# Gate tiles of the retention heads as 2x2 blocks with seven products, the retention's units behind them, and the branch sums kept in memory

## What is computed

```python
h = rmsnorm(x, p['norm_pre_mix']) * (1 + sc1) + sh1
q, k, v, g, xr, gr = jnp.split(h @ p['w_in'], SPLITS, axis=-1)
...
o, s_new = retention(q, k, v, s_ret.astype(f32))     # 4 heads, DK 256, DV 512
o = (o - mu) * lax.rsqrt(var + GN_EPS)
ret_y = (o.reshape(B, T, D_RET_V) * p['ret_gn_w'] * jax.nn.silu(g.astype(f32))).astype(dt)
branch_ret = ret_y @ p['w_br_ret']
...
mixed = (ga * branch_ret + gb * branch_rnn) @ p['w_out']
```

## Time and profile before

| | |
|---|---|
| Median of 3 runs | 1374.01 us (1373.72 to 1374.78) |
| The profiled execution | 1375.0 us, span 1373.2 us |
| PE busy | 1336.7 us (97% of the span), granted clock 0.99 |
| PE weight loads busy | 1263.0 us (92%) |
| DVE busy | 815.3 us (59%) |
| ACT busy | 569.0 us (41%) |
| POOL busy | 206.9 us (15%) |
| DMA | mean 138 GB/s; queue of POOL 44.44 MB, queue of SP 141.80 MB |

### The profile page before, as it was taken

One profiled execution on the slowest core, in us unless ns is written; L12 is line 12 of the kernel. 1 busy time (PEld: TensorE's weight loads), 2 busy tenths in 40 slices (PEclk: granted clock), 3 DMA queues, 4 the chain that ended last, 5 costly groups with the idle time before them and its releaser, 6 DMA issues.

```text
span 1373.2 us, 24780 instructions
## 1 busy us (share of the span) xinstructions
PE 1336.7 (97%) x10380; PEld 1263.0 (92%) x10380; DVE 815.3 (59%) x1159; ACT 569.0 (41%) x847; POOL 206.9 (15%) x324
## 2 busy tenths in 40 slices
PE   6999999999999999999999999999899999999997
PEld 3899999988998898899889898999899999999996
DVE  4559888622353594268437734784787888853223
ACT  4667778211222321232224223426555666543221
POOL 1122232000114122301320131000011121100001
PEclk8999999999999999999999999999999999999998
DMA  9412122583424434524442353227054766743323
GB/s 371 172 62 93 63 77 78 207 334 126 178 77 161 154 109 150 178 90 144 148 159 72 137 181 126 78 78 265 2 165 123 183 165 173 181 126 102 95 85 66
DMA packets 61630, 189.91 MB, mean 138 GB/s; under 512 B 6608, under 2 KB 10192, under 8 KB 61136
## 3 DMA queue, kind: packets, MB, share of 16 engines
q1 hardware_dynamic: 44880, 141.80, 29.9%
q0 software_dynamic: 15488, 44.44, 12.5%
q10 hardware_dynamic: 1152, 2.10, 0.4%
HBM read 164.76 MB, written 23.55 MB: 137 GB/s over the span
## 4 chain that ended last, share of the span: by engine, by line
PE 77%; issue 7%; DVE 7%; DMA 4%; ACT 3%; SPq 1%; POOL 1%; DVEq 0%; ACTq 0%; POOLq 0%
PE ps L935 49%; PE ps L1360 14%; PE ps L944 5%; PE ps L1200 2%; DMA out_rs<-state 1%; PE ps L987 1%; PE ps L1183 1%; DMA ada_raw<-in_w_ada 1%; PE ps L1212 1%; PE ps L1244 1%; PE ps L1230 1%; PE ps L1086 1%; DMA raw<-in_w_out 1%; SPq L846 1%; DVE w_lo L1879 1%
## 5 line engine op out<-in xcount | busy, mean ns | idle before, releaser
L935 PE MATMUL ps<-h_hi,w_hi 128*128 128x272 f32 x1520 | 322.1, 293 | 4.5 <-DVE w_lo L1879 3.7
L935 PE MATMUL ps<-h_hi,w_lo 128*128 128x272 f32 x1520 | 315.3, 289 | 0.0
L935 PE MATMUL ps<-h_lo,w_hi 128*128 128x272 f32 x1520 | 314.5, 288 | 0.0
L1879 DVE TENSOR_TENSOR w_lo<-raw,w_hi 128x1024 fp32r<-128x1024 f32 (+2 forms) x154 | 183.9, 1198 | 190.3 <-ACT w_hi L1445 188.6
L935 PEld LDWEIGHTS ps<-h_hi,w_hi 128*128 128x128 f32 x1520 | 241.0, 189 | 16.3 <-issue 9.0
L1445 ACT ACTIVATE w_hi<-raw 128x1024 fp32r<-128x1024 f32 (+2 forms) x154 | 157.6, 1024 | 216.8 <-PE ps L935 116.9
L935 PEld LDWEIGHTS ps<-h_lo,w_hi 128*128 128x128 f32 x1520 | 239.7, 189 | 0.0
L935 PEld LDWEIGHTS ps<-h_hi,w_lo 128*128 128x128 f32 x1520 | 238.4, 190 | 0.0
L2175 DVE SCALAR_TENSOR_TENSOR state<-state,ps 128x512 f32<-128x512 f32 x64 | 41.0, 682 | 97.5 <-PE ps L1244 97.3
L935 PE MATMUL ps<-a_hi,w_hi 128*128 128x272 f32 x308 | 64.0, 289 | 0.2 <-DVE w_lo L1879 0.2
L2592 POOL DMA_DIRECT2D s_raw<-in_w_fin x18 | 15.6, 865 | 321.7 <-DMA s_raw<-in_w_fin 321.7
(11 more groups left out here) (311 smaller groups left out, 2762.3 us busy)
## 6 DMA issues: line engine op xcount, KB each, us to landing
raw<-in_w_head SPq DMA_DIRECT2D x48, 512.0 KB, 3.9
state<-in_state POOLq DMA_DIRECT2D x32, 512.0 KB, 4.6
out_rs<-state POOLq DMA_DIRECT2D x32, 512.0 KB, 4.4
raw<-in_w_rnn SPq DMA_DIRECT2D x24, 512.0 KB, 3.5
ada_more<-in_w_ada SPq DMA_DIRECT2D x23, 512.0 KB, 7.8
raw<-in_w_fin SPq DMA_DIRECT2D x20, 512.0 KB, 5.4
s_raw<-in_w_fin SPq DMA_DIRECT2D x36, 256.0 KB, 5.6
s_raw<-in_w_fin POOLq DMA_DIRECT2D x36, 256.0 KB, 4.9
```

The lines of the kernel that those rows point to most:

```text
L935: mm = nc.tensor.matmul(dst[:, half, :], a, b[:, half * HALF:(half + 1) * HALF], start=first and j == 0, stop=last and j == 2)
L1879: V.tensor_tensor(lo[:, 0:cols], raw_slab(i)[0][:, 0:cols], hi[:, 0:cols].bitcast(F32), ALU.subtract).then_inc(lo_ready, 1)
```

## The change

The four gate tiles of a head become two *pairs*. A pair is written as a 2x2 block product (two weight tiles by two halves of the columns, with the depth halved as well) and computed with seven products of 12 matmuls each. In this text P1 to P7 are the seven products in PE's order, and pair (h, i) is pair i of head h. P1 and P4 use the slab A, P2 and P5 the slab s13, P3 and P6 the slab s24, P7 the half slab a22. P3 adds into P1's bank, P5 and P7 too, P6 into P2's; ACT copies intermediate results out (`copy_head`) first, so P3 waits for copy 1, P5 and P6 for copy 3, P7 for copy 4.

The sums of weight blocks in s13 are made by two SP loads and two accumulating POOL loads into the one buffer `s_head`; those in s24 by two DVE additions in place, after the low part of s13 has been taken. The sums of the input are made once, in head 0, on DVE and ACT; for them the normalised input is written to memory early (`kept_h`) and read back, and the split sums lie where `gbr` and `acc` lay, so `gbr` is written to memory and the branch sums are kept there too: ACT copies each branch tile to one of 4 buffers (`send`), and POOL sends it to memory with an adding DMA (`add_branch`). Two of these buffers lie in `vf`, where the pairs' copies go as well, and two in `cosin`, which is read again in each head. At the end POOL reads `gbr` and `acc` back.

The units that stood behind g0 and g1 now all stand behind P7 of pair 0, those of g2 and g3 behind P7 of pair 1, on all engines. The diff, cut to its core (SP and the plan, PE, ACT, DVE, POOL):

```diff
+HEAD_PRODUCTS = (("q", "A", 0, "B11"), ("t", "s13", 0, "XC"), ("q", "s24", 0, "XA"), ("s", "A", 1, "B21"),
+                 ("q", "s13", 1, "XB"), ("t", "s24", 1, "B22"), ("q", "a22", 0, "XD"))
+SENT = 4
...
-    return tiles + [("g", e) for e in range(ET)]
+    return tiles + [("pair", i) for i in range(ET // 2)]
...
+        for name, key in slabs.items():
+            pl.add_slab(key, BLOCK if name == "a22" else COLS)
+        for side in range(2):
+            pl.add_tile(("pair", h, i, side))
+        for n, (_, name, _, _) in enumerate(HEAD_PRODUCTS):
+            pl.step(slabs[name])
+            pl.product_end[(h, i, n + 1)] = pl.steps
+        for part in range(2):
+            for u in after[("g", 2 * i + part)]:
+                unit(h, u)
...
+            def load_blocks_of_pair(kind, h, i):
+                below = w["w_head"][h, 8 + 2 * i + 1]
+                if kind == "s13":
+                    if (h, i) != (0, 0):
+                        last = pl.kinds["s24"][pair_number(h, i) - 1]
+                        sp.wait_ge(lo_ready, last + 1)
+                    for s in range(2):
+                        sp.dma_start(s_head[:, s, :], below[:, 0:BLOCK]).then_inc(s_head_in, 16)
+                elif kind == "a22":
+                    if i:
+                        sp.wait_ge(lo_ready, pl.slab[("a22", h, i - 1)] + 1)
+                    else:
+                        sp.wait_ge(q_ready, h + 1)
+                    sp.dma_start(head_a22, below[:, BLOCK:2 * BLOCK]).then_inc(a22_in, 16)
...
+            sp.dma_start(kept_h, x_in[:]).then_inc(h_saved, 16)
...
-            sp.dma_start(cosin[:], w["cosin"]).then_inc(cosin_in, 16)
+            sp.wait_ge(h_saved, again(1))
+            for part in range(2):
+                ks = slice(part * KD // 2, (part + 1) * KD // 2)
+                sp.dma_start(h_again[:, ks, :], kept_h[:, ks, :]).then_inc(h_back, 16)
+                load_to(pl.slab[("v", 0, 2 + part, "w", 0)])
             for h in range(H):
+                load_to(pl.slab[("v", h, ET - 1, "w", 0)])
+                if h:
+                    wait_product(sp, h - 1, 1, PRODUCTS)
+                sp.dma_start(cosin[:], w["cosin"]).then_inc(cosin_in, 16)
...
+            def gate_pair_of_head(h, i, after):
+                for side in range(2):
+                    claim(("pair", h, i, side))
+                slabs, number, used = pair_slabs(h, i), pair_number(h, i), set()
+                for n, (bank, name, side, x) in enumerate(HEAD_PRODUCTS):
+                    pe.wait_ge(lo_ready, pl.slab[slabs[name]] + 1)
+                    if x[0] == "X" and number == 0:
+                        pe.wait_ge(x_ready, ("XC", "XB", "XA", "XD").index(x) + 1)
+                    if n in (2, 4, 5, 6):
+                        pe.wait_ge(gate_copied, 4 * number + {2: 1, 4: 3, 5: 3, 6: 4}[n])
+                    hi, lo, _ = parts_of(pl.slab[slabs[name]])
+                    dst = ps[:, pair_bank(h, i, bank), 0:HALF]
+                    x_hi_block, x_lo_block = x_block(h_hi, hx_hi, x), x_block(h_lo, hx_lo, x)
+                    for k in range(KD // 2):
+                        at = side * BLOCK + k * P
+                        whi, wlo, xh, xl = hi[:, at:at + P], lo[:, at:at + P], x_hi_block[:, k, :], x_lo_block[:, k, :]
+                        for j, (a, b) in enumerate(((whi, xh), (whi, xl), (wlo, xh))):
+                            mm = nc.tensor.matmul(dst, a, b, start=bank not in used and k == 0 and j == 0,
+                                                  stop=k == KD // 2 - 1 and j == 2, skip_group_check=True)
+                    mm.then_inc(multiplied, 1)
+                    used.add(bank)
+                for u in after[("g", 2 * i)] + after[("g", 2 * i + 1)]:
+                    unit(h, u)
...
+            def send(h, m):
+                uses = KD // SENT * h + m // SENT
+                if uses:
+                    act.wait_ge(acc_added[m % SENT], 16 * uses)
+                if m == 0:
+                    act.wait_ge(v3_ready, ET * (h + 2))
+                    act.wait_ge(q_ready, h + 2)
+                evacuate(("br", h, m), sent(m))
+            def all_sent(h):
+                for i in range(SENT):
+                    act.wait_ge(acc_added[i], 16 * (KD // SENT) * h)
...
+            def copy_head(h, i, n, product, bank):
+                wait_product(act, h, i, product)
+                do(A(head_copied(n), ps[:, pair_bank(h, i, bank), 0:HALF], ACT.Copy), gate_copied, wait=False)
+            def gate_pair_of_head(h, i, after):
+                first, number = first_of_pair(h, i), pair_number(h, i)
+                split_to(first + 2)
+                if i == 0:
+                    act.wait_ge(q_ready, h + 1)
                     if h:
-                        act.wait_ge(r_ready, ET * h)
-                    evacuate(key, gs[:, i, :], ACT.Silu)
+                        all_sent(h)
+                    else:
+                        act.wait_ge(v3_ready, ET)
+                split_to(first + 3)
+                copy_head(h, i, 0, 1, "q")
+                copy_head(h, i, 1, 2, "t")
+                copy_head(h, i, 2, 3, "q")
+                split_to(first + 4)
+                copy_head(h, i, 3, 5, "q")
+                act.wait_ge(*took(("pair", h, i, 1)))
+                do(A(gs[:, 2 * i, :], gs[:, 2 * i, :], ACT.Silu), wait=False)
+                act.wait_ge(gate_row, number + 1)
+                below = gs[:, 2 * i + 1, :]
+                do(A(below[:, HALF:T], below[:, HALF:T], ACT.Silu, scale=-1.0), wait=False)
+                wait_product(act, h, i, PRODUCTS)
+                do(A(below[:, 0:HALF], ps[:, pair_bank(h, i, "q"), 0:HALF], ACT.Silu, scale=-1.0),
+                   *took(("pair", h, i, 0)), wait=False)
+                split_to(first + 5)
+                for u in after[("g", 2 * i)] + after[("g", 2 * i + 1)]:
+                    unit(h, u)
...
+            def ahead_in_branch(h, m):
+                split_to(pl.slab[("br", h, m // 2, "w")] + (1 if m == KD - 2 else AHEAD))
...
                 for name, i in head_tiles(h):
-                    if name == "br":
-                        split_to(pl.slab[("br", h - 1, i // 2, "w")] + AHEAD)
+                    if name == "pair":
+                        gate_pair_of_head(h, i, after)
+                    elif name == "br":
+                        if i < KD - 1:
+                            ahead_in_branch(h - 1, i)
+                        send(h - 1, i)
+                        if i == KD - 1:
+                            ahead_in_branch(h - 1, i)
                     else:
...
+            def gate_pair_of_head(h, i, after):
+                first, number = first_of_pair(h, i), pair_number(h, i)
+                split_to(first + 1)
+                s2, s4, upper = s_head[:, 0, :], s_head[:, 1, :], raw_slab(first)[0]
+                dve.wait_ge(lo_ready, first + 2)
+                do(V.tensor_tensor(s2, s2, upper[:, 0:BLOCK], ALU.add))
+                do(V.tensor_tensor(s4, s2, upper[:, BLOCK:2 * BLOCK], ALU.add), sums_ready)
+                split_to(first + 3)
+                t = gs[:, 2 * i, :]
+                dve.wait_ge(gate_copied, 4 * number + 1)
+                wait_product(dve, h, i, 4)
+                do(V.tensor_tensor(t[:, 0:HALF], head_copied(0), ps[:, pair_bank(h, i, "s"), 0:HALF], ALU.add))
+                split_to(first + 4)
+                dve.wait_ge(gate_copied, 4 * number + 3)
+                wait_product(dve, h, i, 6)
+                do(V.tensor_tensor(t[:, HALF:T], head_copied(2), ps[:, pair_bank(h, i, "t"), 0:HALF], ALU.add),
+                   *took(("pair", h, i, 1)))
+                dve.wait_ge(gate_copied, 4 * number + 4)
+                do(V.tensor_tensor(gs[:, 2 * i + 1, HALF:T], head_copied(3), head_copied(1), ALU.add), gate_row)
+                split_to(first + 5)
+                units(h, after[("g", 2 * i)] + after[("g", 2 * i + 1)])
...
+            def add_blocks(h, i):
+                pool.wait_ge(s_head_in, again(2 * pair_number(h, i) + 2))
+                pool.dma_start(s_head[:, 0, :], w["w_head"][h, 8 + 2 * i + 1][:, BLOCK:2 * BLOCK], accum_op=ALU.add)\
+                    .then_inc(s_head_added, 16)
+                pool.dma_start(s_head[:, 1, :], w["w_head"][h, 8 + 2 * i][:, 0:BLOCK], accum_op=ALU.add)\
+                    .then_inc(s_head_added, 16)
+            def add_branch(h, m):
+                wait_took(pool, ("br", h, m))
+                if h:
+                    pool.dma_start(kept_acc[:, m, :], sent(m), accum_op=ALU.add).then_inc(acc_added[m % SENT], 16)
+                else:
+                    pool.dma_start(kept_acc[:, m, :], sent(m)).then_inc(acc_added[m % SENT], 16)
...
+                if h == 0:
+                    add_blocks(0, 0)
...
                         load_state(u + 2)
+                    if h:
+                        for m in {1: (0, 1, 2, 3), 2: (4, 5), 3: (6, 7)}.get(b, ()):
```

(24 more changed lines are left out.)

167 lines of the change are left out of this document (126 added, 41 removed).

## The result

The changed kernel takes 1440.2 us in the median (1439.6 to 1441.9), the kernel before 1373.9 us in the same runs: a ratio of 1.048, 95% interval 1.047 to 1.050. The forecast was 1430.5 us, range 1396 to 1447. The profiled execution has a span of 1437.8 us, 64.6 us more than before.

The account below looks back on a forecast made before the run. PE was taken as the bound, busy 130.09 of head 1's 131.0 us. Terms -12.0 + 8.4 + 23.4 + 3.6 + 9.9 + 16.2 + 7 = +56.5 on 1375.0 gave 1431.5, median 1430.5 us, range 1396 to 1447.

Parts of the forecast that it names:

- Saving: All 8 pairs: 84 matmuls instead of 96 each, 96 fewer at 0.1254 us, 12.0 us saved.
- Weight sums: Pair 1 of all heads: P3 waits for s2, s4 and the split of s24, 2.1 us each, 8.4 us.
- Branch sums: Pair 0 of heads 1 to 3: P3 waits for ACT's copy behind the landing sums, 7.8 us each, 23.4 us.
- Rival 1: POOL's transfers don't queue up; pair 0 of heads 1 to 3 waits only 2.1 us: 1410 us, chance 0.18.
- Bank wait behind b3: Behind pair 0 of heads 1 to 3: o3 waits for b3's first PSUM bank, 1.2 us each, 3.6 us.
- Row at a head's end: b5, p3, b6, os, b7 in a row: 7.95 us against 4.7, 3.3 more three times, 9.9 us.
- Head 0: Waits at pair (0,0) 5.6 us, behind it 4.7 us, row at the head's end 5.9 us: together 16.2 us.
- Clock: New heads: waits of 5 us and more, about five, lower PE's clock, 1.4 us each: 7 us (0 to 13).
- 2 (a slower queue, about 1446): POOL's queue is slower than taken and every wait over 3 us lowers the clock: about 1446 us, chance 0.10.
- 4 (no gaps): The seven products run without a gap as in the FFN: 1362 us, chance 0.06.
- 3 (only the weight sums): Row ends, banks and head 0 find cover; only 8 pairs wait 2.1 us each: 1379 us, chance 0.07.

Follow-up runs that it names:

- e12: e11 with, in pair 0 of heads 1 to 3, fs also between P2 and P3, nothing between P5 and P6, p2 also behind P7: 1370.5 us, ratio 0.998.
- e2: Changed kernel with DVE forming s2 and s4 early: pair 0's (heads 1 to 3) before b2's update, pair 1's right behind its slabs' split: 1441.2 us.
- e4: Changed kernel with all branch sums as plain writes that add nothing (sums of heads 1 and 2 missing from the result): 1436.6 us.
- e1: Changed kernel with ACT's copies of a pair's first three products waiting only for br4 and br5; wait for br6, br7 and a22's split behind them: 1446.4 us.
- e6: e1 with the next pair's s13 split only behind o2 and o3 (ACT) or b3 (DVE), in head 0 behind sc and b0: 1420.9 us.
- e5: Changed kernel with a pair's first unit list between P2 and P3 and the second between P5 and P6: 1392.6 us, ratio 1.014.
- e9: e5 with b7's key block before state 5's store, and b4 (head 0: b3) behind pair 0's P7, os and b7 behind pair 1's: 1377.4 us, ratio 1.002.
- e11: e9 with s2 and s4 earlier, PE's second PSUM bank pair claimed before P2, and head 0's p3, b6, os, b7 behind P7: 1373.8 us, ratio 0.999.

## Why the prediction was right, and where it was not

- **The size and its mechanism** were right: 1440.2 against 1430.5, PE's waits in the heads as named, head 1 143.7 us long (144 said), head 0 16.0 us longer (15 said). That the total came so near is in part luck, for it is the sum of two errors of opposite sign: 61.5 us of waits were forecast, 49.7 measured; 7 us of clock, 26.9 measured.
- **Saving.** 96 matmuls went, as said; e12 shows the 3 us of a head as real once nothing waits.
- **Weight sums, 2.1 us each.** 2.35, 2.34, 2.35 and, in head 0, 1.87 us: right. With the clock behind each wait 3.8 (e2).
- **Branch sums, 7.8 us three times.** Measured 2.7, 6.3 and 6.3. P3 was to start 10.8 us into the pair and started 5.9 us into it in head 1. The 4.9 us between them come of three parts: the store of state 1 went out 9.0 us before the pair and not 7.3; the load behind it followed after 7.4 us, as in the earlier trace rows, and not after 8.9, so the two sums ahead of it in the queue cost it nothing more; and the last sum landed 6.1 us after that load's issue, not 8.0. In heads 2 and 3 the extra came from the adding write (e4), which the prediction priced like a plain one, with 0 to 6 us more in the range. Rival 1 needed a store of 4.4 us and a sum of 4.1. Head 1 had 6.5 and 4.7, and its wait lies nearer to the rival's 2.1 than to the forecast; heads 2 and 3 lie near the forecast. By the fit of the Trainium skill, "DMA: Bandwidth & Descriptors", Anatomy of one DMA, a sum would land in 2.6 us, an estimate from its figures; 4.7 (plain) and 6.6 us (adding) were measured.
- **The terms were added as if each could be had by itself.** They can't: e1 freed 10.3 us and lost 16.4, e2 freed 15 and lost as much. What stood behind the branch sums was the reload of `s_head`, which the prediction used for pair (0,0) and left out for the other heads. It didn't ask of the waits that the change adds what is late next once one of them goes.
- **Bank wait behind b3, 1.2 us.** 1.0 in all three heads. Right, and e6 shows its cause, the split ahead of the units.
- **Row at a head's end, 7.95 us.** 9.5: the chain as said, the rest low clock and POOL's last two steps, 1.42 and 1.07 us here beside 0.39 and 0.73 at 581 us. Each ends 0.3 and 0.6 us after one of DVE's additions that runs beside it (until 609.17 and 610.01), so POOL seems to wait for these. All traces here bear it out: each of the 64 casts and subtractions of this kind that start while DVE works on two inputs in SBUF ends 0.25 or 0.6 us after DVE's instruction, and takes longer than the 0.39 or 0.73 us of all the others, 211 of which start beside a DVE instruction with an input in PSUM. The Trainium skill ("SBUF — State Buffer", Who interferes with whom) says so: a DVE instruction with two inputs in SBUF contends with one of GpSimd that reads SBUF. The times agree; no run took the additions away.
- **Head 0, 16.2 us of waits.** The head came out 16.0 us longer, but its parts are wrong: PE's idle time rose by 10.3 us (from 1.2 to 11.5), and 8.7 are clock, less the 3.0 saved. State 7's load cost 3.9 (3.7 said), but o01 waited 1.2 and not 4.7, and the split of s24 held P3 by 2.4, with 1.84 before P1, where 5.6 were said.
- **Clock, 7 us.** This is the term that was mis-sized. It was counted for waits of 5 us and more. The trace shows the 1.2 GHz level after 2.35 us too, in each pair, and at each v0. The Trainium skill ("TensorE: Matmul & The Clock Gate", Why this matters for your kernels) was quoted for the few long waits; its rule speaks of longer gaps than those before P3 of pair 1, and where it and the traces differ, the traces decide.
- **Rivals.** 2 (a slower queue, about 1446) gave the total a little better than the forecast, but not by its mechanism: the queue was quicker than forecast, and only its dearer clock came. 4 (no gaps) needs the units as cover: e12 comes within 0.6 us of its head 1. 3 (only the weight sums) is excluded by the changed kernel's waits, 26 us of them on ACT's copies and the key block, and by e2, where pair 1's weight sums stopped waiting and the time stayed.

## What to carry to other kernels

When an engine is full, a fast algorithm saves its share only if each operand is ready at its turn: put the work that used to stand between the old tiles between the new products, one piece before the first product that needs a late operand and one behind the last, before the next owner of its PSUM banks. Waits behind one another hide each other: before a cause is priced, follow the chain past it to the next resource, above all to buffers that one transfer must leave before the next may enter. And price idle time of PE with the clock behind it, here 1.4 to 1.7 us for each us of waiting.

## What the runs showed of the hardware

- Idle time and clock go together over all kernels. By the profiled executions, more PE idle time than before (36.5 us) against more time for the same matmuls (1324.7 us at the clock of before): changed kernel 49.7 and 26.9; e6 36.8 and 21.1; e5 19.3 and 13.6; e9 12.7 and 8.4; e11 7.6 and 3.6. All but e12 have 0.4 to 0.7 us of clock for each us of waiting; e12 has 4.8 and 4.3. A wait of 1.86 us cost 1.5 us of clock in one pair of e6 and none in two others.
- A write of 272 KB that adds into memory, against a plain one, over the twelve kernels with pairs: POOL's issue of two takes 1.87 us instead of 1.13, and the landing 7.1 us in the median (5.4 to 10.9) instead of 5.6 (3.3 to 8.0). A 512 KB store behind two adding writes landed in 7.1 to 8.0 us, behind two plain ones in 5.7 to 7.3. With none of POOL's DMAs still under way it took 3.2 us in the median (3.1 to 6.2).
- A cast of POOL's takes 0.39 us, but 0.73 to 1.47 when it starts while DVE works on two inputs in SBUF; the subtraction behind it 0.73, and 0.81 to 1.75.
